# Fetching experts before the latent mLSTM cells are done: moving cells beside the first expert pairs

## The reference

```python
x = x + g1[:, None, :] * (jnp.concatenate([m_out, a_out], axis=-1) @ w_out)
h2 = modulate(rmsnorm(x, n2), sh2, sc2)
# peer(h2): q = h2 @ w_q; top 16 of each half's scores; top 16 of the 256 sums; gates = softmax
a = jax.nn.gelu(jnp.einsum('pd,phkd->phk', xb, u_tab[eb]))
out = jnp.einsum('phk,phkd->pd', gb * a, v_tab[eb])
```

## Time and profile before

| | us |
|---|---|
| median of 3 runs | 3685.37 |
| lowest and highest | 3685.03, 3698.58 |
| span of the profiled execution | 3682.8 |
| first expert fetch issued, from the span's start | 664.1 |

### The profile page before, as it was taken

One profiled execution on the slowest core, in us unless ns is written; L12 is line 12 of the kernel. 1 busy time (PEld: TensorE's weight loads), 2 busy tenths in 40 slices (PEclk: granted clock), 3 DMA queues, 4 the chain that ended last, 5 costly groups with the idle time before them and its releaser, 6 DMA issues.

```text
span 3682.8 us, 31091 instructions
## 1 busy us (share of the span) xinstructions
PE 2644.4 (72%) x9770; PEld 1042.0 (28%) x9770; DVE 2453.7 (67%) x5523; ACT 990.0 (27%) x2700; POOL 1459.0 (40%) x1300
## 2 busy tenths in 40 slices
PE   7999888687877878866566567557656755775655
PEld 3455567333333333312121112112111211221111
DVE  3666435776787678648857677685767768576655
ACT  1223333442433244422122122212212221221111
POOL 0110023443454455434444444444444444444443
PEclk9999889899989989889799789879977987987677
DMA  7222446899999999999999999999999999999999
GB/s 299 95 97 94 163 125 204 333 410 422 416 421 426 425 412 420 389 424 414 427 427 427 427 423 427 422 417 424 416 427 420 427 420 423 424 417 427 411 427 380
DMA packets 224537, 1365.12 MB, mean 371 GB/s; under 512 B 25194, under 2 KB 36074, under 8 KB 75890
## 3 DMA queue, kind: packets, MB, share of 16 engines
q0 software_dynamic: 165888, 1208.03, 78.4%
q1 hardware_dynamic: 50992, 134.74, 10.1%
q10 hardware_dynamic: 7492, 20.36, 1.4%
HBM read 1334.05 MB, written 28.99 MB: 370 GB/s over the span
## 4 chain that ended last, share of the span: by engine, by line
DMA 40%; PE 20%; DVE 15%; issue 4%; POOL 4%; ACT 4%; SPq 0%; ACTq 0%; POOLq 0%; DVEq 0%
DMA fx_ring<-arg_uv,fx_eidx 38%; PE fx_acc L1396 11%; DVE fx_ring L1846 8%; POOL fx_ring L1109 4%; PE at_sP L1241 3%; ACT fx_weighted_pick L1542 2%; PE at_aP L1203 1%; DMA rt_wq<-arg_w_q 1%; DVE rt_rest L1708 1%; DVE rt_ab L1710 1%; DVE rt_rest L1706 1%; DMA rt_w_q<-arg_w_q 1%; PE at_sP L1269 1%; ACT fx_gelu L1538 1%; PE at_sP L1187 1%
## 5 line engine op out<-in xcount | busy, mean ns | idle before, releaser
L1396 PE MATMUL fx_acc<-fx_ring,fx_weighted_pick 128*64 128x512 f32 x4608 | 1417.7, 747 | 929.8 <-ACT fx_weighted_pick L1542 908.3
L1109 POOL DMA_INDIRECT fx_ring<-arg_uv,fx_eidx x1152 | 1317.0, 1143 | 1634.7 <-PE fx_acc L1396 1444.5
L1846 DVE CUSTOM_DVE_ANT_0 fx_ring<-fx_ring,fx_h 128x1024 f32<-128x1024 f32 x1152 | 1411.8, 1237 | 774.0 <-DMA fx_ring<-arg_uv,fx_eidx 769.5
L1396 PEld LDWEIGHTS fx_acc<-fx_ring,fx_weighted_pick 128*64 128x64 f32 x4608 | 327.0, 158 | 1903.7 <-ACT fx_weighted_pick L1542 1368.4
L1538 ACT ACTIVATE fx_gelu<-fx_dot 128x2 f32<-128x2 f32 x576 | 117.1, 203 | 2116.2 <-DVE fx_dot L1846 2115.7
L424 PE MATMUL in_z<-w_in,in_hT 128*128 128x512 f32 (+1 forms) x864 | 352.4, 566 | 7.3 <-PEq L97 7.3
L1542 ACT ACTIVATE fx_weighted_pick<-fx_weighted_pick,fx_gelu 128x64 f32<-128x64 f32 x1152 | 338.0, 340 | 55.1 <-ACT fx_gelu L1538 2.2
L424 PEld LDWEIGHTS in_z<-w_in,in_hT 128*128 128x128 f32 x864 | 163.6, 192 | 177.3 <-issue 172.0
L1269 PE MATMUL rt_qP<-rt_w_q,rt_h2T 128*128 128x512 f32 x384 | 193.6, 629 | 9.4 <-DMA rt_w_q<-arg_w_q 9.4
L384 POOL COPY in_turned<-in_heads 128x320 f32<-128x320 f32 x9 | 9.1, 1010 | 320.1 <-DVE in_heads L579 320.1
L1241 PE MATMUL at_sP<-at_w_out,at_mixT 128*128 128x512 f32 x288 | 133.3, 606 | 0.9 <-DVE at_mixT L1601 0.9
(11 more groups left out here) (300 smaller groups left out, 2450.4 us busy)
## 6 DMA issues: line engine op xcount, KB each, us to landing
rt_wq<-arg_w_q SPq DMA_DIRECT2D x44, 512.0 KB, 7.8
fx_ring<-arg_uv,fx_eidx POOLq DMA_INDIRECT x1152, 12.7
in_ada_w<-arg_w_ada SPq DMA_DIRECT2D x32, 512.0 KB, 4.0
ml_qkT<-qkT_scratch SPq DMA_DIRECT2D x18, 512.0 KB, 4.2
ada_w<-arg_w_ada SPq DMA_DIRECT2D x8, 1024.0 KB, 13.8
w_in<-arg_w_in SPq DMA_DIRECT2D x16, 512.0 KB, 16.4
rt_w_q<-arg_w_q SPq DMA_DIRECT2D x16, 512.0 KB, 32.7
kv_scratch<-in_kv ACTq DMA_DIRECT2D x9, 768.0 KB, 3.3
```

The lines of the kernel that those rows point to most:

```text
L1109: pool.indirect_dma_start(out=ring[j][:], out_offset=None, in_=io.uv, in_offset=bass.IndirectOffsetOnAxis(ap=eidx[t % 2][:, i:i + 1], axis=0),
L1396: mm = pe.matmul(acc[b][cg * TOKS:(cg + 1) * TOKS, :], wsel[:, i % (2 * FILL), :], ring[i % GROUP][:, D + b * 512:D + (b + 1) * 512], star ...
L1846: dve.tensor_tensor_reduce(out=ring[j][:, 0:D], in0=ring[j][:, 0:D], in1=h2r[t % 2][cg][:], scale=1.0, scalar=0.0, op0=ALU.mult, op1=ALU.a ...
```

## The change

The cells' work is split over the time before and after the first fetches. Beside route steps 6 to 33 of tile 0 one cell step runs at every third step. `begin` now comes before the cells are done: POOL waits for tile 0's stored x1 and issues the first four pairs' fetches (each still waits for the choice, `s_route`). Three cell steps follow, and 25 more run one beside each of tile 0's pairs 0 to 24 (`CELL_PAIRS`). The mixers of tiles 1 to 8 start at pair 25 of tile 0 (`due`), the route of tile 1 starts at pair 40 with one and two steps in turn (`pace`).

For this tile 0's mixer has buffers of its own (`first`), and the later mixers' buffers (`later`) and w_q lie over the mLSTM's state, so W_out is loaded and scaled twice, and tile 1's q and mask, gate1 and W_out are loaded by SP at mixer 1's first piece, after all h are stored. The PSUM banks are exchanged: tile 0's mixer and route use `acc`, the cells `other`. On PE, mixer 1 waits for the last cell, and `begin` for the transposed queries of both halves of tile 0 and its h2 rows.

```diff
     def due(t, r):
+        if t == 0:
+            return r >= CELL_PAIRS
         if t == STREAMED - 1:
             return r < WQ_AT
-        return t == 0 and r < SUBS or 17 <= r < 23 or r >= 51 or r % 2
+        return r < 25 or r >= 51 or r % 2
 
     def pace(t, r):
+        if t == 0:
+            return int(r < 17) if r < CELL_PAIRS + SUBS else 1 + r % 2
...
     def cells_beside(k):
         if k < TURN:
             return 1
-        if k < TURN + 11:
-            return int(k % 3 > 0)
-        return 1 + int(k % 4 > 0)
+        return int(k % 3 == 0)
...
             next(steps)
-        for _ in cells:
-            pass
         begin()
+        for _ in range(3):
+            next(cells)
...
+                if t == 0 and r < CELL_PAIRS:
+                    next(cells, None)
+                if t == 0 and r == CELL_PAIRS - 1:
+                    for _ in cells:
+                        pass
                 if due(t, r):
...
+        later = mixer_buffers(1)
+        with ExitStack() as room:
+            w_q = room.enter_context(nc.sbuf_tensor("rt_w_q", [P, KD, 2 * D], F32))
+        held = sb("mixer_room", [P, ROOM])
+        first = mixer_buffers(0)
...
-        eP = acc[0][:].rearrange("p (h n) -> p h n", n=P)
+        eP = other[0][:].rearrange("p (h n) -> p h n", n=P)
...
+        first.ST, later.ST = acc, other
+        qP0, cP0 = acc, aP[:].rearrange("p (h n) -> p h n", n=P)
...
+                def load_weights(cnd):
+                    m = later if cnd else first
+                    sp.dma_start(m.gate1[:], g.gate_dram[cnd:cnd + 1, :].to_broadcast([P, D])).then_inc(s_g1, 16)
+                    for k in range(KD):
+                        sp.dma_start(m.w_out[:, k, :], io.w_out[k * P:(k + 1) * P, :]).then_inc(s_wo, 16)
...
+                        if k == 0 and t == 1:
+                            load_head(1)
+                            load_weights(1)
...
-                        if k == 10 and t + 1 < TILES:
+                        if k == 10 and 0 < t < TILES - 1:
                             load_head(t + 1)
...
                 def begin():
-                    pool.wait_ge(s_hd, UNITS)
-                    for d in range(2):
-                        pool.wait_ge(s_hst[d], 16 * TILES)
+                    pool.wait_ge(s_x1o, 16)
                     for n in range(DEPTH):
                         fetch(n)
...
                     if t == 1:
-                        pe.wait_ge(s_qT, NG)
                         pe.wait_ge(s_cs, NG)
-                        pe.wait_ge(s_h2a, NC)
-                        pe.wait_ge(s_h2d, NC)
+                        pe.wait_ge(s_n, UNITS * 2)
+                        pe.wait_ge(s_cn, UNITS * 4)
...
                 def begin():
-                    pe.wait_ge(s_hd, UNITS)
+                    pe.wait_ge(s_qT, NG)
+                    pe.wait_ge(s_h2d, NC)
...
-                        if 5 <= k < 5 + KD // 2 and t == 0:
+                        if 5 <= k < 5 + KD // 2 and t < 2:
                             j = k - 5
-                            dve.wait_ge(s_wo, 16 * KD)
-                            dve.tensor_scalar(w_out[:, j, :], w_out[:, j, :], mhg[:, j:j + 1], None, ALU.mult).then_inc(s_wom, 1)
+                            dve.wait_ge(s_wo, 16 * KD * (t + 1))
+                            dve.tensor_scalar(m.w_out[:, j, :], m.w_out[:, j, :], mhg[:, j:j + 1], None, ALU.mult).then_inc(s_wom, 1)
```

More of the change, by code:

```diff
@@ L675, in mix_and_experts @@
     LOW = -3.0e38
+    ROOM = 17640
+    CELL_PAIRS = 25
     def tiles(t):
@@ L770, in mix_and_experts, with mixer_buffers, esb @@
         g.state.close()
+        def mixer_buffers(n):
+            with ExitStack() as room:
+                def esb(name, shape, dt=F32):
+                    return room.enter_context(nc.sbuf_tensor(f"{name}_{n}", shape, dt))
+                m = Names()
+                m.w_out = esb("at_w_out", [P, KD, D])
+                m.aq = esb("at_qT", [P, AH // 2, P])
+                m.mask = esb("at_mask", [P, 4 * P])
+                m.gate1 = esb("at_gate1", [P, D])
+                m.s = [esb(f"at_s{i}", [P, 4 * P]) for i in range(2)]
+                m.pT = [esb(f"at_pT{i}", [P, 4 * P]) for i in range(2)]
+                m.nmx = esb("at_negmax", [P, AH])
+                m.rs = esb("at_sum", [P, AH])
+                m.es = esb("at_sink_exp", [P, AH])
+                m.hq = esb("at_h_square", [P, MW])
+                m.sg = esb("at_sigmoid", [P, MW])
+                m.hr = esb("at_hrms", [P, MH])
+                m.mix = esb("at_mix", [P, D])
+                m.hs = m.mix[:, 0:MW]
+                m.mixT = esb("at_mixT", [P, KD, P])
+                m.x1 = esb("at_x1", [P, D])
+                m.xn = esb("at_xn", [P, D])
+            return m
+        later = mixer_buffers(1)
+        with ExitStack() as room:
+            w_q = room.enter_context(nc.sbuf_tensor("rt_w_q", [P, KD, 2 * D], F32))
+        held = sb("mixer_room", [P, ROOM])
+        first = mixer_buffers(0)
         ring = [sb(f"fx_ring{i}", [P, 2 * D]) for i in range(GROUP)]
@@ L804, in mix_and_experts @@
         gex = sb("rt_gexp", [P, PH, TOPK])
[L806 to L833, removed]
+        wq = wq2 + h2r[0]
         acc = [psum(f"fx_acc{i}") for i in range(2)]
-        ST = [psum(f"at_sP{i}") for i in range(2)]
+        other = [psum(f"at_sP{i}") for i in range(2)]
         aP = psum("at_aP")
@@ L941, in load_head @@
                 def load_head(t):
+                    m = first if t == 0 else later
                     if t:
                         sp.wait_ge(s_sc, t * AH)
-                    sp.dma_start(aq[:].rearrange("p h n -> p (h n)"), g.aqT_dram[t]).then_inc(s_q, 16)
+                    sp.dma_start(m.aq[:].rearrange("p h n -> p (h n)"), g.aqT_dram[t]).then_inc(s_q, 16)
                     if t in (0, 1, 2, TILES - 1):
@@ L947, in load_head @@
                             sp.wait_ge(s_nm, t * AH)
-                        sp.dma_start(mask[:], io.att_mask[t]).then_inc(s_mk, 16)
+                        sp.dma_start(m.mask[:], io.att_mask[t]).then_inc(s_mk, 16)
                 def load_h(t):
+                    m = first if t == 0 else later
                     if t < 2:
@@ L1068, in _ @@
                 load_head(0)
[L1069 to L1072, removed]
+                sp.dma_start(first.x1[:], io.x[0]).then_inc(s_x, 16)
+                load_weights(0)
                 for m in range(2 * WQ):
@@ L1434, in route @@
                     for k in range(steps_of(t)):
-                        x1t = x1r if t else x1[:]
+                        x1t = x1r if t else first.x1[:]
                         if k == TURN - 3:
@@ L1811, in begin @@
                 def begin():
-                    for d in range(2):
-                        dve.wait_ge(s_hst[d], 16 * TILES)
+                    pass
                 def close(t):
```

131 lines of the change are left out of this document (69 added, 62 removed).

## The result

The change makes the kernel slower: 3752.2 us in the median of 4 runs (3744.7 to 3756.7) against 3690.0 (3685.0 to 3698.6), a ratio of 1.0171 (1.0148 to 1.0194), some 63 us. The forecast was 3695, and its range ended at 3728.

What follows compares the result with a forecast made beforehand. Compute waits bound the kernel up to 664.1 us, then DMA bytes at 419 GB/s. Span 3682.8 - 50 + 36 + 8 + 2 + 14 = 3692.8 us, plus 2.6 to the median: 3695 us, range 3664 to 3728.

Steps and rivals of the forecast that it cites:

- Term 1: Start of the expert fetches: first fetch at 614 us (607 to 624), a gain of 50 us (40 to 57).
- Term 2: Bytes moved behind the first fetch: 14.9 MB more, 36 us at 419 GB/s (33 to 45).
- Other edits: New buffers, exchanged PSUM banks, column views: no instruction's size changes; scaling w_out again stays under the transfers, 3 us if late.
- From tile 3 on nothing changes: Sign named in advance: the stretch from tile 3 to the end stays as in the kernel before.
- the ledger: Whole kernel: end = start of the fetches + bytes after it / rate + DMA time left idle after it.
- Term 3: DMA time left idle after the first fetch: 8 us beside cells, 2 at tile 1's loads, 14 in pairs 40 to 63.
- The cell stage: Tile 0's pairs 0 to 24, one cell step each: 8 us of idle DMA (0 to 20), share 0.93 to 1.01.
- the handover: Pair 25 of tile 0, waits for tile 1's h, q, mask, gate and w_out: 2 us idle (0 to 8).
- The dense pairs 40 to 63: Tile 0 pairs with mixer pieces and tile 1's route: 14 us idle (0 to 35), 155 to 170 us, share 0.88 to 0.96.
- eight rounds: Query weight loops in tile 0's pairs 40 to 63: 9.6 us of transfers against about 10.5 each, 9 us idle.
- TensorE becomes the bound: Rival, chance 0.32: tile 0's pairs 40 to 63 need more than 148 us of transfers; at its upper bound 3716 us.
- threshold of 171 us: Tile 0's pairs 40 to 63: the slower rival decides from 23 us of extra idle time, 7.1 us a pair.

Runs made afterwards that it cites:

- aligned: Changed kernel with 96 bytes of small tables allocated ahead of the ring, so its slots begin at byte 99328, a multiple of 1024: 3719.0 us, ratio 1.0081.
- second loads: Changed kernel's buffers, banks and repeated loads of w_out, gate, q and mask, in the old order, ring on its boundary: 3703.1 us, ratio 1.0036.
- short weight loads: Changed kernel with the ring on its boundary, loading only the first eighth of the columns of tile 1's query weight chunks: 3707.1 us in one execution.

## Why the prediction was wrong

The 63 us part as follows. The ring's address is 0.90% (after less aligned), 33 us, seen again as 0.98% and 1.06% in the kernel before. The second loads are 0.36%, 13 us. The order is 0.45% (aligned less second loads), 17 us net, which is the gain of the start and its price in one. The ratios have intervals of 0.13 to 0.23 points to either side, and their differences some 0.3, 10 us; the address and the order are clear of that.

**Term 1, start 614 (gain 50).** Right: 616.1, a gain of 48, and for the reason given. VectorE starts the choice at 566.2 us (forecast 566) and finishes the cell behind half 1's query from 600.5 to 602.9 us (forecast 603), with 12 us of choice behind it. Between, it waits 4.6 and 1.8 us for products that stand behind queries in TensorE's order, so this path costs some 6 us at most.

**Term 2, 14.9 MB, 36 us.** Right in the bytes: 14.7 MB. Of the time, only the second loads were priced by themselves, 13 us for 12 forecast; for the cells' 9.7 MB no run shows a price.

**Other edits: "New buffers, exchanged PSUM banks and column views change no instruction's size."** This is the step that failed. It is true of the instructions' sizes, but it left the packets that land in these buffers out. With it fell "From tile 3 on nothing changes". The term was forecast at 0 and measured 33 us by taking it away, and 36 by adding it to the kernel before. No bound was set for it: the ledger took the rate of 419 GB/s from the kernel before as a constant, and no rival let it move.

**Term 3, idle DMA.** The cell stage was right: the fetches of pairs 0 to 23 at a share of 0.99 to 1.03, 6.0 us a pair, and the handover took little (0.95 in eight pairs, 2 to 3 us). The dense pairs 40 to 63 were mis-sized, and this is the second step that failed. Forecast 155 to 170 us at 0.88 to 0.96; measured 191.5 us (fetch 40 at 862.1, tile 1's first at 1053.6), with 0.70 in the last eight pairs. TensorE was summed at 142 us, 153 at a granted clock of 0.93; in the aligned kernel it is busy for 39.3 + 54.3 + 73.0 = 167 us at a clock of 0.90 over the three stretches, and 28 more pass while it waits. By the same division, an estimate, 142 us at 0.90 are 158, so 5 of the 14 us above the forecast are clock and 9 are work not counted. The forecast spread the work evenly, and so did not see that the last third of the stretch carries the choice, the second query, h2's rows and the mixer at once (TensorE 73 and VectorE 61 of 86 us), while the first third has a share of 1.01 in the changed kernel and 0.96 in the aligned one. It also missed that the choice ends at pair 62 and is due at 60; this wait of 18 us shrinks when mixer pieces leave the stretch, and nothing was gained where it was removed by denser route steps.

**The terms together.** With the measured sizes, and with 148 us for the dense pairs' transfers, an estimate of the prediction, the ledger closes: -48 for the start, 35 for 14.7 MB at 419 GB/s, 2 for the handover, 43 for the dense pairs above their transfers and 33 for the address make 65 us, and 63 were measured. By the forecast's own sum, the address alone would have led to 3695 + 33 = 3728, the end of the range; without it the aligned kernel stands at 3719, within the range. It took both errors to leave it.

**The sums.** Two don't come out as written. The upper bound, worked out from its terms (start 624, dense stretch 35), is 3726 and not 3728; eight rounds that each take 0.9 us longer than their transfers make 7 us and not 9. Neither changes the outcome.

**The rivals.** No rival let the rate move, so none gives the measured time. Without the address term the kernel takes 3719 us, and "TensorE becomes the bound" gave 3716: its threshold of 171 us for the 24 pairs was passed by 20. As to the order, it was the case that came true, at 0.32; the forecast of 14 us of idle time was too low. The name is half right. With short weight loads TensorE is busy 157 of 179 us, so it is the longest engine, yet in the last eight pairs it is busy 65 of 74 us, and several engines wait for each other there. That they form one chain is argued from these waits and not shown by a run.

The prediction weighed two figures of the Trainium skill, page "DMA: Bandwidth & Descriptors", and neither entered its sum. The time of one DMA, under "Anatomy of one DMA", is fitted there for transfers that GpSimd issues, while the weight chunks are issued by SP; their landings in 5.0 and 8.1 us stand as measured. Against the limit of a core of about 358 GB/s, under "Specifications", stand 423 GB/s with the ring on a boundary and 417 off it.

What stays open: which boundary between 128 and 1024 bytes suffices, and by what mechanism the address costs time; and why two and one and a half cell steps a pair lose about as much as they win, of which only the waits are known.

## What to carry to other kernels

A kernel bound by its DMA can have an address term, as this one has. When an allocation moves, compare the bytes a second at equal share in a stretch whose work did not change. Keep the targets of the large transfers on the boundary on which they were fast, here a multiple of 1024 bytes; 96 bytes of small tables ahead of the ring were enough for it. Work moved behind a full queue gains only the idle time it leaves less the bytes it brings, here 48 us less 35, and a few pairs with three streams in them are enough to lose the rest. So sum each engine over thirds of a stretch, not over the whole. Price a move of buffers by itself, in the old order, before the order is changed.

## What was not expected of the hardware

The start address of the ring's slots within a partition changed the time of the 8 KB packets of the fetches, which read rows of the same table. The median was 309 ns at a multiple of 1024, with 1% of the packets at 319 ns or more. It was 312 ns at 64 and at 160 above a multiple of 256, with 20% and 13% of them at 319 ns or more. In rates that is 423 against 417 GB/s over 1300 us. Shifts of 64 and of 160 bytes cost the same within the intervals, 1.06% and 0.98% of the kernel.
